# Weight casts on ScalarE: one by one in the norms, four in the cross attention, token-major copies ahead of squares

## The chip, the cores and the metric

The kernel runs on one core of a Trainium2 chip. The metric is the device time of one execution in microseconds (us); smaller is better. Three runs of the kernel before took 1008.64, 1008.8 and 1011.63 us, so the median is 1008.8 us.

The engines are TensorE (PE in the profile, with PEld for its weight loads), VectorE (DVE), ScalarE (ACT), GpSimd (POOL) and SyncE (SP), which only issues transfers here. Each works through its own instructions in order, and waits on semaphores for the others.

## The reference

Two transformer blocks run one after the other on 256 tokens of width 1024, in fp32:

```
first block:   u = rms_norm(h); proj = u @ w_in
               y_a = softmax attention of 8 heads (RoPE)          [moba, att]
               y_b = gated delta rule of 8 heads, in chunks       [conv, tok, feat, inv, scan]
               h += rms_norm((sig(ga)*(y_a@w_proj_a) + sig(gb)*(y_b@w_proj_b)) @ w_out)     norm "mix"
               h += rms_norm((silu(f@w_gate) * (f@w_up)) @ w_down)                          norm "ffn1"
               h += sigmoid(h @ w_ple_gate) * e                                             norm "ple"
second block:  x += rms_norm(concat(diff attention, pooling) @ w_out_2)                     norm "mix2"
               x += rms_norm(cross_attention(rms_norm(x)@w_xq, mem) @ w_xo)                 norm "x"
               x += rms_norm((silu(f@w_gate_2) * (f@w_up_2)) @ w_down_2)                    norm "ffn2"
```

The names at the right are the kernel's for the places where a product's rows are normed, added to the residual and made ready for the next product. The gated delta rule needs its q and k normed over the 128 dimensions of a head, so their squares are summed; `tok` is the step that does it.

## The kernel before, in words

Each fp32 product is computed in three passes: weights and activations are split into a high and a low half (`w_hi`, `w_lo`, `uH`, `uL`), and PE computes high x high (L505), high x low weight (L506) and low x high weight (L507). The 2 x 128 tokens (t = 0, 1) are the stationary side, 512 columns of weights the moving side; the results lie in eight PSUM banks, L0 to L3 for the large products and Q0 to Q3 for turned (transposed) tiles.

The weights come as 294 units of 128 x 1024 numbers (512 KB). Every unit takes four stations:

- SP loads it into one of four `raw` places. Unit n waits until the low half of unit n - 4 is made, since that frees its place.
- ACT casts it to `w_hi` (L1257). This cast waits for the load, and for PE to be done with the unit that held the `w_hi` place before.
- POOL subtracts, two instructions a unit, to `w_lo` (L495).
- PE uses it.

The order of all this is written out by hand. `schedule()` lists the steps, and each engine's function goes through them. ACT does the casts between its other work, at the points where the code says `split_past`, `split_up_to` or `split_freed`. `split_freed(step, j)` makes all casts that need no more of PE than that unit j of that step is used up; for what was already made it does nothing. What the code puts behind such a call waits, on ACT, until those casts are done, and so for their loads.

A norm between two products is spread over three engines. The names below are those of the code, each for token tile t and column half c:

- ACT `row_sum` squares a PSUM bank and sums it (L1348, tile `hg`; in norm "ple" it is a sigmoid on L1346). It waits for the bank.
- DVE `gained` (L1885), `root` (L1818, seven small instructions), `added` (L1903) and `scaled` (L1914, writes `hg`).
- PE `turn_half` turns that half (L722, four instructions).
- ACT `kept` copies the residual out of PSUM (L1332), and `hi_half` casts the turned half to `uH` (L1269). DVE `lo_half` subtracts to `uL` (L1851). The next product's matmuls on this half (L505) wait for it, in `wait_low`; `bank_free` makes them wait for `kept` too.

PE calls the first `turn_half` of a norm just ahead of the last nine matmuls of the product before it (`row_tail`, TAIL = 5 units for t = 1). These nine are the only work that PE has while ACT and DVE do the high and the low half.

In the cross attention (`cross`), ACT copies turned probabilities (`cross_probs`, L1320) and casts the attention's output to `uH` (`cross_hi`, L1326), while PE computes values and already a part of `xo`, the product behind it. In `tok`, PE turns 3 parts (q, k, v) x 2 token tiles through banks Q0 to Q2 (L920), ACT copies each out (L1450) and squares q and k (L1459), and DVE sums the squares (L2010). A bank is turned into again when its copy is out.

Of the kernel before, what the change touches and what calls it, by code (L numbers as in the profile page):

```python
# [26 lines left out]
ACT = mybir.ActivationFunctionType  # L27
# [4 lines left out]
NT = SEQ // P  # L32
# [3 lines left out]
GH = 4  # L36
# [125 lines left out]
TAIL = 5  # L162
# [57 lines left out]
def build(nc, a, out, known):  # L220
# [30 lines left out]
    with ctx:  # L251
# [986 lines left out]
        def _(act):  # L1238
# [146 lines left out]
            def fill(step, i):  # L1385

                split_up_to(FIRST[FILLING[step][0]] + i + SPLIT)
# [5 lines left out]
            for step in SCHEDULE:  # L1393
# [50 lines left out]
                elif kind == "tok":  # L1444
                    for part in range(3):
                        for t in range(NT):
                            act.wait_ge(*PE(step, "turned", part, t))
                            if part == 0 and t == 0 and step[1] == 1:
                                act.wait_ge(*PE(("scan", 0), "o", 1))
                            copy(tok[:, t, part, :, :], Q[(part * NT + t) % 3][:].rearrange("p (h d) -> p h d", h=GH)).then_inc(*AC.mark(step, "out", part, t))  # L1450
                            if t == 0:
                                fill(*((step, part - 1) if part else (("decay", step[1]), 3)))
                            if part < 2:
                                act.wait_ge(*AC(step, "out", part, t))
                                if part > 0:
                                    act.wait_ge(*VE(step, "sum", part - 1, t))
                                elif step[1] == 1:
                                    act.wait_ge(*VE(("scan", 0), "sum", t))
                                actf(sq[t][:], tok[:, t, part, :, :], ACT.Square).then_inc(*AC.mark(step, "sq", part, t))  # L1459
                    fill(step, 2)  # L1460
# [141 lines left out]
                elif kind == "norm":  # L1602
# [6 lines left out]
                    if what == "ffn2":  # L1609
                        row_sum(what, 2)  # L1610
                        row_sum(what, 3)
                        continue
                    split_freed(src_step, last - 3)
                    if pre:
                        kept(what, 0, 0)
                elif kind == "next":
# [3 lines left out]
                    pre = RES[what][1]  # L1620
                    hi_half(step, 0, 0)
                    row_sum(what, 2)
                    row_sum(what, 3)
                    if pre:
                        kept(what, 0, 1)
# [150 lines left out]
                elif kind == "cross":  # L1776
# [9 lines left out]
                    cross_hi(0)  # L1786
                    cross_probs(1)
                    cross_hi(1)
                elif kind == "xo":
# [610 lines left out]
```

## Time and profile before

| | |
|---|---|
| median of three runs | 1008.8 us |
| the profiled execution | 1008.19 us |
| its span, first to last instruction | 1006.4 us |
| PE busy | 974.2 us, 97% |
| POOL busy | 741.9 us, 74% |
| ACT busy | 512.1 us, 51% |
| DVE busy | 366.0 us, 36% |
| mean granted clock of PE | 0.994 of full speed |

The span covers the program's instructions; some 1.8 us lie around it. "Busy" is time in which an engine executes something; a matmul's end is modelled, so that rows of consecutive matmuls overlap. In a timeline row the figure in brackets is how long the engine sat idle before the row, with what ended that.

### The profile page before, as it was taken

How to read it: one execution, taken by the hardware profiler on the slowest of the kernel's cores; microseconds unless marked ns; L12 is line 12 of the kernel's file. 1: busy time of each engine (PE TensorE's matmuls, PEld its weight loads, DVE VectorE, ACT ScalarE, POOL GpSimd, SP SyncE). 2: the span in 40 equal slices, each digit the busy share in tenths (PEclk: the TensorE clock that was granted, in tenths of full speed). 3: DMA queues.
4: the chain of work that ended last, by engine and by line, in shares of the span. 5: the costliest groups of instructions: out<-in, count | busy, mean ns of one | idle time of the engine just before them, and what ended most of it. 6: DMA issues, size and time to landing. Idle time of an engine off the chain costs nothing.

```text
span 1006.4 us, 15320 instructions
## 1 busy us (share of the span) xinstructions
PE 974.2 (97%) x6004; PEld 830.0 (82%) x6004; DVE 366.0 (36%) x840; ACT 512.1 (51%) x759; POOL 741.9 (74%) x592
## 2 busy tenths in 40 slices
PE   5999999999999999999999998999999899999997
PEld 5988889988888887888898876899888778888885
DVE  4677434776524235112122244143253161111103
ACT  5376624465524446465444554575556465444431
POOL 6868543876632987999976976868976579888890
PEclk9999999999999999999999999999999999999999
DMA  8546231555332775667654665645655357666541
GB/s 262 177 129 206 85 112 61 179 154 167 106 107 84 235 246 167 212 201 210 189 167 148 195 205 166 220 149 170 190 189 164 95 159 227 188 189 187 180 136 42
DMA packets 76752, 167.37 MB, mean 166 GB/s; under 512 B 8348, under 2 KB 13704, under 8 KB 76552
## 3 DMA queue, kind: packets, MB, share of 16 engines
q1 hardware_dynamic: 71296, 156.40, 50.6%
q10 hardware_dynamic: 5384, 9.99, 3.0%
q8 instruction: 47, 0.77, 0.3%
q14 instruction: 25, 0.20, 0.1%
HBM read 165.32 MB, written 1.05 MB: 165 GB/s over the span
## 4 chain that ended last, share of the span: by engine, by line
PE 84%; POOL 5%; ACT 3%; DVE 3%; DMA 2%; issue 1%; DVEq 0%; ACTq 0%
PE L L505 19%; PE L L507 19%; PE L L506 18%; POOL w_lo L495 5%; PE L L865 2%; PE Q L507 2%; PE Q L505 2%; PE Q L506 2%; PE L L867 2%; PE L L866 2%; ACT w_hi L1257 1%; PE Q L1034 1%; PE Q L1016 1%; PE Q L722 1%; DMA raw<-in_w_in 1%
## 5 line engine op out<-in xcount | busy, mean ns | idle before, releaser
L495 POOL TENSOR_TENSOR w_lo<-raw,w_hi 128x512 fp32r<-128x512 f32 x588 | 741.7, 1299 | 238.9 <-ACT w_hi L1257 238.3
L1257 ACT CAST w_hi<-raw 128x1024 fp32r<-128x1024 f32 x294 | 304.9, 1053 | 259.6 <-PE L L507 103.9
L505 PE MATMUL L<-w_hi,uH 128*128 128x512 f32 (+1 forms) x768 | 306.0, 398 | 6.3 <-DVE uL L1851 6.0
L507 PE MATMUL L<-w_hi,uL 128*128 128x512 f32 (+1 forms) x768 | 297.3, 387 | 0.0
L506 PE MATMUL L<-w_lo,uH 128*128 128x512 f32 (+1 forms) x768 | 296.8, 386 | 0.0
L505 PEld LDWEIGHTS L<-w_hi,uH 128*128 128x128 f32 x768 | 145.1, 189 | 37.8 <-DVE uL L1851 9.5
L507 PEld LDWEIGHTS L<-w_hi,uL 128*128 128x128 f32 x768 | 144.8, 189 | 30.0
L506 PEld LDWEIGHTS L<-w_lo,uH 128*128 128x128 f32 x768 | 145.2, 189 | 27.0 <-issue 0.5
L505 PE MATMUL L<-w_hi,hH 128*128 128x512 f32 x176 | 69.0, 392 | 0.0
L507 PE MATMUL L<-w_hi,hL 128*128 128x512 f32 x176 | 68.6, 390 | 0.0
L506 PE MATMUL L<-w_lo,hH 128*128 128x512 f32 x176 | 68.5, 389 | 0.0
L1812 DVE TENSOR_TENSOR hL<-Q,hH 128x512 fp32r<-128x512 f32 x22 | 15.2, 692 | 121.3 <-ACT hH L1669 120.9
L865 PE MATMUL L<-uH,w_hi 128*128 128x256 f32 x192 | 55.0, 287 | 0.9 <-DVE baH L1969 0.8
L866 PE MATMUL L<-uL,w_hi 128*128 128x256 f32 x192 | 54.4, 284 | 0.0
L867 PE MATMUL L<-uH,w_lo 128*128 128x256 f32 x192 | 54.4, 283 | 0.0
L1885 DVE TENSOR_TENSOR L<-L,gA 128x512 f32<-128x512 f32 x20 | 14.0, 699 | 97.3 <-ACT hg L1348 96.8
L1818 DVE TENSOR_SCALAR small<-small 128x1 f32<-128x1 f32 (+1 forms) x177 | 39.0, 220 | 24.1 <-ACT xv L1593 13.1
L1851 DVE TENSOR_TENSOR uL<-Q,uH 128x512 fp32r<-128x512 f32 x28 | 19.3, 691 | 64.3 <-ACT uH L1269 64.3
L1821 DVE SCALAR_TENSOR_TENSOR hm<-L,small,sil 128x512 f32<-128x512 f32 x20 | 15.0, 751 | 65.7 <-PE L L507 65.3
L507 PEld LDWEIGHTS L<-w_hi,hL 128*128 128x128 f32 x176 | 33.0, 188 | 7.0
L506 PEld LDWEIGHTS L<-w_lo,hH 128*128 128x128 f32 x176 | 33.1, 188 | 6.7
L505 PEld LDWEIGHTS L<-w_hi,hH 128*128 128x128 f32 x176 | 33.1, 188 | 6.6
(335 smaller groups left out, 1281.8 us busy)
## 6 DMA issues: line engine op xcount, KB each, us to landing
raw<-in_w_in SPq DMA_DIRECT2D x88, 512.0 KB, 3.6
raw<-in_w_ffn_gate SPq DMA_DIRECT2D x22, 512.0 KB, 3.7
raw<-in_w_ffn_up SPq DMA_DIRECT2D x22, 512.0 KB, 3.7
raw<-in_w_ffn_down SPq DMA_DIRECT2D x22, 512.0 KB, 3.5
raw<-in_w_gate SPq DMA_DIRECT2D x22, 512.0 KB, 3.6
raw<-in_w_up SPq DMA_DIRECT2D x22, 512.0 KB, 3.6
raw<-in_w_down SPq DMA_DIRECT2D x22, 512.0 KB, 3.5
raw<-in_w_out SPq DMA_DIRECT2D x16, 512.0 KB, 3.5
```

The costliest lines, as they stand in the source:

```text
L495: last = nc.gpsimd.tensor_tensor(lo[:, cc], raw[:, n % RAW, cc], hi[:, cc].bitcast(F32), ALU.subtract)
L505: mm(dst, sH, wH, start=start, stop=False)
L506: mm(dst, sH, wL, start=False, stop=False)
L507: return mm(dst, sL, wH, start=False, stop=stop)
L865: mm(bank, sH, uH[:, k, :], start=k == 0, stop=False)
L866: mm(bank, sH, uL[:, k, :], start=False, stop=False)
L867: last = mm(bank, sL, uH[:, k, :], start=False, stop=k == KD - 1)
L1257: copy(halves[SLOT[u]][0], raw[:, u % RAW, :]).then_inc(w_hi_there, 1)
L1812: v(V.tensor_tensor(out_, x_, y_, op), *name)
L1818: v(V.tensor_scalar(out_, x_, s1, s2_, op0, op1), *name)
L1821: v(V.scalar_tensor_tensor(out=out_, in0=x_, scalar=s_, in1=y_, op0=op0, op1=op1), *name)
L1851: vector_next(V.tensor_tensor(uL[:, 4 * half:4 * half + 4, t * P:(t + 1) * P], heads(Q[2 * t + half]), uH[:, 4 * half:4 * half + 4, t * P: ...
```

## The change

Three edits, all in the ACT function. PE, DVE, POOL and SP keep their instructions and their order.

1. `tok`: the copies and squares, written as a loop before, are written out. The copy of (part 1, t 0) now stands ahead of the squares of (part 0, t 1), where it stood behind.
2. The norms: `split_freed(src_step, last - 3)` ahead of the first `kept` made three casts in a row. Now `last - TAIL` makes one there; the second stands behind the first `hi_half`, and the third behind the row sums of t = 1. This holds for the norms "mix", "ffn1", "ple", "mix2" and "x"; "ffn2", the last, has no casts.
3. `cross`: `split_freed(values, 3)` is added between the second `cross_probs` and the second `cross_hi`. It makes four casts, which the step `xo` made before.

```diff
--- before.py
+++ after.py
@@ -1442,21 +1442,33 @@
                         if t == 0:
                             fill(step, 2)
                 elif kind == "tok":
-                    for part in range(3):
-                        for t in range(NT):
-                            act.wait_ge(*PE(step, "turned", part, t))
-                            if part == 0 and t == 0 and step[1] == 1:
-                                act.wait_ge(*PE(("scan", 0), "o", 1))
-                            copy(tok[:, t, part, :, :], Q[(part * NT + t) % 3][:].rearrange("p (h d) -> p h d", h=GH)).then_inc(*AC.mark(step, "out", part, t))
-                            if t == 0:
-                                fill(*((step, part - 1) if part else (("decay", step[1]), 3)))
-                            if part < 2:
-                                act.wait_ge(*AC(step, "out", part, t))
-                                if part > 0:
-                                    act.wait_ge(*VE(step, "sum", part - 1, t))
-                                elif step[1] == 1:
-                                    act.wait_ge(*VE(("scan", 0), "sum", t))
-                                actf(sq[t][:], tok[:, t, part, :, :], ACT.Square).then_inc(*AC.mark(step, "sq", part, t))
+                    def token_major(part, t):
+                        act.wait_ge(*PE(step, "turned", part, t))
+                        if part == 0 and t == 0 and step[1] == 1:
+                            act.wait_ge(*PE(("scan", 0), "o", 1))
+                        copy(tok[:, t, part, :, :], Q[(part * NT + t) % 3][:].rearrange("p (h d) -> p h d", h=GH)).then_inc(*AC.mark(step, "out", part, t))
+
+                    def squares(part, t):
+                        act.wait_ge(*AC(step, "out", part, t))
+                        if part > 0:
+                            act.wait_ge(*VE(step, "sum", part - 1, t))
+                        elif step[1] == 1:
+                            act.wait_ge(*VE(("scan", 0), "sum", t))
+                        actf(sq[t][:], tok[:, t, part, :, :], ACT.Square).then_inc(*AC.mark(step, "sq", part, t))
+
+                    token_major(0, 0)
+                    fill(("decay", step[1]), 3)
+                    squares(0, 0)
+                    token_major(0, 1)
+                    token_major(1, 0)
+                    squares(0, 1)
+                    fill(step, 0)
+                    squares(1, 0)
+                    token_major(1, 1)
+                    squares(1, 1)
+                    token_major(2, 0)
+                    fill(step, 1)
+                    token_major(2, 1)
                     fill(step, 2)
                     fill(step, 3)
                 elif kind == "moba":
@@ -1610,7 +1622,7 @@
                         row_sum(what, 2)
                         row_sum(what, 3)
                         continue
-                    split_freed(src_step, last - 3)
+                    split_freed(src_step, last - TAIL)
                     if pre:
                         kept(what, 0, 0)
                 elif kind == "next":
@@ -1619,8 +1631,10 @@
                     last = KF if src_step[0] == "down" else KD
                     pre = RES[what][1]
                     hi_half(step, 0, 0)
+                    split_freed(src_step, last - TAIL + 1)
                     row_sum(what, 2)
                     row_sum(what, 3)
+                    split_freed(src_step, last - TAIL + 2)
                     if pre:
                         kept(what, 0, 1)
                     hi_half(step, 0, 1)
@@ -1785,6 +1799,7 @@
                     values_out(3, [Q[2], Q[3]])
                     cross_hi(0)
                     cross_probs(1)
+                    split_freed(values, 3)
                     cross_hi(1)
                 elif kind == "xo":
                     split_freed(step, KD - TAIL - 1)
```

How the change moves instructions, as the two programs' ACT orders show it (a number behind an x is how often the row repeats; numbers behind `w_hi` name a tile outside the first six places).

First the norm "mix". `hg,small<-L` are the row sums, `h<-L` is `kept`, `uH<-Q` is `hi_half`. Before:

```order
L1348 ACTIVATE hg,small<-L 128x512 x2
L1257 CAST w_hi<-raw 128x1024 x3
L1332 COPY h<-L 128x512
L1269 CAST uH<-Q 128x4x128
L1348 ACTIVATE hg,small<-L 128x512 x2
L1332 COPY h<-L 128x512
L1269 CAST uH<-Q 128x4x128
```

After:

```order
L1348 ACTIVATE hg,small<-L 128x512 x2
L1257 CAST w_hi<-raw 128x1024
L1332 COPY h<-L 128x512
L1269 CAST uH<-Q 128x4x128
L1257 CAST w_hi<-raw 128x1024
L1348 ACTIVATE hg,small<-L 128x512 x2
L1257 CAST w_hi<-raw 128x1024
L1332 COPY h<-L 128x512
L1269 CAST uH<-Q 128x4x128
```

Two of three casts have moved behind the first high half, one of them on behind the second pair of row sums. "ffn1" (which has no `kept`), "ple" and "mix2" move alike.

Second the end of the cross attention, `xo` and the norm "x". The first row is `cross_hi` of t = 1 before, the first cast after; the tiles 130 and 132 are places lent from the memory's buffers. Before:

```order
L1326 CAST uH<-Q 128x4x128 x2
L1257 CAST w_hi<-raw 128x1024 x2
L1257 CAST w_hi_130<-raw 128x1024
L1257 CAST w_hi_132<-raw 128x1024
L1257 CAST w_hi<-raw 128x1024 x2
L1257 CAST w_hi_138<-raw 128x1024
L1348 ACTIVATE hg,small<-L 128x512 x2
L1257 CAST w_hi_140<-raw 128x1024
L1257 CAST w_hi<-raw 128x1024 x2
L1332 COPY h<-L 128x512
L1269 CAST uH<-Q 128x4x128
```

After:

```order
L1257 CAST w_hi<-raw 128x1024 x2
L1257 CAST w_hi_130<-raw 128x1024
L1257 CAST w_hi_132<-raw 128x1024
L1326 CAST uH<-Q 128x4x128 x2
L1257 CAST w_hi<-raw 128x1024 x2
L1257 CAST w_hi_138<-raw 128x1024
L1348 ACTIVATE hg,small<-L 128x512 x2
L1257 CAST w_hi_140<-raw 128x1024
L1332 COPY h<-L 128x512
L1269 CAST uH<-Q 128x4x128
L1257 CAST w_hi<-raw 128x1024
L1348 ACTIVATE hg,small<-L 128x512 x2
```

Seven casts stood between `cross_hi` and the norm's row sums; now three do, and four stand ahead of `cross_hi`.

Third the start of `tok`, group 0. `tok<-Q` is a copy, `sq<-tok` a square. Before:

```order
L1450 COPY tok<-Q 128x512
L1459 ACTIVATE sq_90<-tok 128x512
L1450 COPY tok<-Q 128x512
L1459 ACTIVATE sq_91<-tok 128x512
L1450 COPY tok<-Q 128x512
L1257 CAST w_hi<-raw 128x1024
```

After:

```order
L1449 COPY tok<-Q 128x512
L1457 ACTIVATE sq_90<-tok 128x512
L1449 COPY tok<-Q 128x512 x2
L1457 ACTIVATE sq_91<-tok 128x512
L1257 CAST w_hi<-raw 128x1024
```

The third copy has moved ahead of the second square.

## Rows read from the trace of the kernel before

**Rows 1.** The page: span, and the busy time of PE

```profile
span 1006.4 us, 15320 instructions
PE 974.2 (97%) x6004; PEld 830.0 (82%) x6004; DVE 366.0 (36%) x840; ACT 512.1 (51%) x759; POOL 741.9 (74%) x592
```

**Rows 2.** Waits of PE, whole span: line, waited for, us in total, times, longest

```profile
PE L L505 <- DVE uL L1851: 6.0, 4, 2.8
PE Q L722 <- DVE hg L1914: 5.4, 2, 5.0
```

**Rows 3.** Timeline of PE, idle rows: start, us, what, [idle <-releaser]

```profile
75.48 0.63 PE L920 MATMUL Q<-table,C 128*128 128x128 f32 x4 [0.51 <-ACT tok L1450]
...
388.57 0.50 PE L505 MATMUL L<-w_hi,uH 128*128 128x512 f32 x1 [1.85 <-DVE uL L1851]
...
585.10 0.50 PE L505 MATMUL L<-w_hi,uH 128*128 128x512 f32 x1 [1.10 <-DVE uL L1851]
...
611.90 0.50 PE L505 MATMUL L<-w_hi,uH 128*128 128x512 f32 x1 [2.78 <-DVE uL L1851]
...
807.21 1.11 PE L722 MATMUL Q<-table,hg 128*128 128x128 f32 x4 [5.03 <-DVE hg L1914]
...
811.70 0.50 PE L505 MATMUL L<-w_hi,uH 128*128 128x512 f32 x1 [0.30 <-DVE uL L1851]
```

**Rows 4.** Timeline of PE, norm "mix": the turned half

```profile
384.02 0.60 PE L722 MATMUL Q<-table,hg 128*128 128x128 f32 x4
```

**Rows 5.** Timeline of ACT, norm "mix": third cast, high half

```profile
385.70 1.05 ACT L1257 CAST w_hi<-raw 128x1024 fp32r<-128x1024 f32 x1 [1.01 <-DMA raw<-in_w_ffn_up]
...
387.13 0.59 ACT L1269 CAST uH<-Q 128x512 fp32r<-128x512 f32 x1
```

**Rows 6.** Timeline of POOL, norms "mix", "ple", "mix2"; two instructions are a unit

```profile
376.95 15.01 POOL L495 TENSOR_TENSOR w_lo<-raw,w_hi 128x512 fp32r<-128x512 f32 x12 [3.81 <-ACT w_hi L1257]
...
599.36 14.97 POOL L495 TENSOR_TENSOR w_lo<-raw,w_hi 128x512 fp32r<-128x512 f32 x12 [4.75 <-ACT w_hi L1257]
...
734.52 1.30 POOL L495 TENSOR_TENSOR w_lo<-raw,w_hi 128x512 fp32r<-128x512 f32 x1 [1.34 <-ACT w_hi L1257]
```

**Rows 7.** Windows: length, busy of PE, PEld, DVE, ACT, POOL, granted clock, DMA share, GB/s

```profile
612.00:615.00 3.00, 3.00 (x11) 2.35 (x11) 1.84 (x3) 0.61 (x2) 2.33 (x2) 0.57 0.60 219
615.00:618.00 3.00, 3.00 (x14) 2.44 (x13) 1.98 (x3) 2.71 (x4) 1.09 (x1) 0.86 0.60 186
...
807.20:811.70 4.50, 4.20 (x13) 3.20 (x13) 1.44 (x3) 3.04 (x7) 4.50 (x5) 0.65 0.74 217
```

**Rows 8.** Timeline of ACT, cross attention to norm "x"

```profile
778.51 1.08 ACT L1320 COPY cpT<-Q 128x512 f32<-128x512 f32 x2
786.82 0.59 ACT L1326 CAST uH<-Q 128x512 fp32r<-128x512 f32 x1 [7.23 <-PE Q L840]
...
789.09 3.89 ACT L1257 CAST w_hi<-raw 128x1024 fp32r<-128x1024 f32 x4
796.36 1.05 ACT L1257 CAST w_hi<-raw 128x1024 fp32r<-128x1024 f32 x1 [3.38 <-DMA raw<-in_w_gate]
...
802.33 0.58 ACT L1348 ACTIVATE hg<-L 128x512 f32<-128x512 f32 x1
```

**Rows 9.** Timeline of POOL, cross attention to the next product

```profile
768.22 7.52 POOL L495 TENSOR_TENSOR w_lo<-raw,w_hi 128x512 fp32r<-128x512 f32 x6 [3.12 <-ACT w_hi L1257]
790.22 24.86 POOL L495 TENSOR_TENSOR w_lo<-raw,w_hi 128x512 fp32r<-128x512 f32 x20 [14.49 <-ACT w_hi L1257]
```

**Rows 10.** Timeline of ACT, norm "mix2": first row sum

```profile
722.40 0.60 ACT L1348 ACTIVATE hg<-L 128x512 f32<-128x512 f32 x1 [4.00 <-PE L L507]
```

**Rows 11.** Timeline of PE, norm "mix2": its first turned half

```profile
727.65 0.60 PE L722 MATMUL Q<-table,hg 128*128 128x128 f32 x4
```

**Rows 12.** Timeline of ACT, `tok` of group 0: second square, third copy

```profile
74.23 0.63 ACT L1459 ACTIVATE sq<-tok 128x512 f32<-128x512 f32 x1
74.77 0.57 ACT L1450 COPY tok<-Q 128x512 f32<-128x512 f32 x1
```

## The prediction, on record before the kernel after was run

> **What bounds the kernel now.** I read four views. The page comes first: PE is busy 974.2 of 1006.4 us [rows 1], so only its 32 idle us can be won by a change that leaves PE's instructions as they are. Second the waits of PE: apart from the start and the end of the kernel, it waits 6.0 us for low halves `uL` and 5.4 us for normed rows `hg` [rows 2]; low weight halves from POOL are not among PE's waits. Third the timeline of PE, which places them: 0.51 us in `tok`, then 1.85, 1.10 and 2.78 us in the norms "mix", "ffn1" and "ple", each just before the next product's first matmul, and in the norm "x" 5.03 us before its first turned half and 0.30 us behind it [rows 3]. These six are 11.6 us. Fourth the timelines of ACT and POOL around them, for what ACT did meanwhile.
>
> **The high half behind three casts.** In "mix" PE turned the first half from 384.02 to 384.62 [rows 4]. ACT could have cast it then, but its third weight cast stood ahead: it waited for a load until 385.70, and the high half began at 387.13 [rows 5]. `uL` came 1.4 us later, and PE, out of work at 388.57 - 1.85 = 386.72, went on at 388.57 [rows 3]. In the changed order one cast stands ahead, and it is made while DVE still works on the rows. The high half starts at about 384.65, 2.5 us earlier, and `uL` is there at 387.13 - 2.5 + 1.4 = 386.05, 0.7 us before PE needs it. So the 1.85 us go. "ffn1" and "ple" have the same pattern, with waits of 1.10 and 2.78 us. In "ple" the third cast waited for its load longest, so the most goes there; PE starts its turn, as in "mix" (386.72 - 384.02), 2.7 us before it runs dry, and the turn, the hand-over, the high and the low half need 0.6 + 0.05 + 1.4 = 2.05 us of that. In "mix2" PE shows no such wait, and I put 0 there. Sum of the norms' low-half waits: 1.85 + 1.10 + 2.78 = 5.73 us.
>
> **The four casts.** ACT is idle for 7.23 us ahead of the first `cross_hi` of t = 1 at 786.82, and behind the second one it makes four casts in 3.89 us from 789.09 [rows 8]. POOL, with nothing to subtract, has been idle for 14.49 us by 790.22 [rows 9], and as only its subtraction frees a `raw` place, the loads stand still too: the fifth cast waits 3.38 us for its load [rows 8]. With two more such waits behind it, ACT comes to the row sums at 802.33 [rows 8]. How late is that? In "mix2", where no cast stands in the way, row sum and turned half begin at 722.40 and 727.65, 5.25 us apart [rows 10, 11]. In "x" PE was ready to turn at 807.21 - 5.03 = 802.18, so its row sum could have begun at 802.18 - 5.25 = 796.9; it began 5.4 us late, which is the wait of 5.03 us [rows 3]. In the new order the four casts start when `cross_probs` ends, at 779.6, and end at 783.5, 3.3 us ahead of `cross_hi` at 786.82 [rows 8]. All four loads are there: POOL made three units from 768.22 to 775.74 [rows 9], and the last load was free to start when it ended, 6.7 us before the fourth cast begins at 782.5. POOL goes from 780.7, at 2.49 us a unit (24.86 us for 10 [rows 9]), and has made four units by 790.7. The three casts that still stand ahead of the row sums need loads that start at 783.2, 785.7 and 788.2 and the first three `xo` units used up by PE, the last of them at about 794.5 (eleven pieces of three matmuls follow it before 802.18; nine matmuls took 386.72 - 384.62 = 2.1 us in "mix", so these take 7.7). They end by 796, the row sum begins near 796.9, and the 5.03 us go. The 0.30 us behind are again a high half behind two casts, and go as in "mix".
>
> **The clock.** After the two longest waits PE's granted clock is down: 0.57 of full speed in 612 to 615, 0.86 in 615 to 618, 0.65 in 807.2 to 811.7 [rows 7], that is, 1.2 GHz for part of each window and 2.4 for the rest. That cost 3.0 x 0.43 + 3.0 x 0.14 = 1.7 us in "ple" and 4.5 x 0.35 = 1.6 us in "x". Where the wait is gone the fall should be gone: 3.3 us. After 1.85 and 1.10 us the windows show nothing to win.
>
> The Trainium skill ("TensorE: Matmul & The Clock Gate", section "What's actually happening") speaks against counting on this: the activity window runs free of the kernel, so when the clock changes differs from run to run. By that rule a fall can come at another wait of the changed kernel, or have been missing in some runs of the kernel before. The trace has one execution and can't show which.
>
> **`tok`.** PE's turn at 75.48 waited 0.51 us for the copy at 74.77, which stood behind the square of 74.23 [rows 3, 12]. The copy moves up by the square's 0.54 us and the wait goes. The square and its sum on DVE come 0.5 us later; the next square waits for its own copy behind a cast anyway, so this costs nothing. If DVE's sums were on the path it would be 0.5 us a group, and the edit worth 0. Group 1 shows no wait: 0.
>
> **What the moved casts may cost.** Each cast that moves back is hidden only while POOL still has units in hand. In "mix" POOL runs six units without a pause from 376.95 in 15.01 us [rows 6], 2.50 us each, so it takes the fifth (the cast that moves behind the high half) at 386.95; the cast will end at about 386.2. The margin is 0.75 us. In "ple" it takes its fifth at 599.36 + 10.0 = 609.3 [rows 6], and the cast ends near 608.6: 0.7 us. PE needs that unit's low half about 0.5 us after it is made, in "mix" and in "ple". In "mix2" the cast comes some 3 us later than now, after POOL has run out, so POOL falls back 1.8 us; but it idles 1.34 us before 734.52 [rows 6], and PE uses that unit some 3 us after it is made. Cost 0 at the forecast. The other new thing is that the second residual copy and high half now stand behind a cast of 1.05 us [rows 5]. PE and the next DVE steps had 0.4 to 0.7 us to spare there by my count. I take 0.1 us for each of four norms, 0.4 in all; the bounds are 0 and 1.05 x 4 = 4.2 us. Below nothing it can hardly go, except that the first matmul after a wait takes 0.50 us [rows 3], longer than those behind it: I allow 0.1 us at five places.
>
> **Sum.** 0.51 + 5.73 + 5.03 + 0.30 + 3.3 - 0.4 = 14.5 us, all on PE's own path. The profiled execution took 1008.19 us, 0.6 under the median of 1008.8, so 993.7 in its terms and 994.3 us for the median.
>
> **The rivals.**
> - *The waits move one place on.* The second high half, now behind a cast, or the residual copy that frees its bank, makes PE wait instead. For it: the margins of half a microsecond. Against it: the cast is short and its load is already there. Price up to 4.2 us: 998.5.
> - *The four casts don't help "x".* Their loads or places come late, or the three casts left still reach the row sums. For it: the loads there have been the slowest of all, 3.38 us [rows 8]. Against: that wait followed from POOL's pause, which goes. Then 5.03 + 0.30 + 1.6 = 6.9 us are missing: 1001.2.
> - *The clock falls somewhere all the same.* The time is 3.3 us longer: 997.6.
> - *The change doesn't do what it says.* The one cast left ahead of the copies waits as long as the three did. That cast needs only the unit that PE uses up first behind the row sums, well before the turn, so this is unlikely. Only the 0.51 us and "x" remain: 1001.
> - *Slower: POOL runs dry.* Two casts are moved back in each norm. If each reached POOL too late for PE, PE would wait at most for one cast and two subtractions, 1.05 + 2.50 = 3.55 us [rows 5, 6]; twice in four norms that is 28.4 us, so 994.3 + 28.4 = 1022.7. It decides from 14.5 / 8 = 1.8 us per moved cast. The margins of 0.7 us ahead of POOL and 0.5 behind it would have to be wrong by 3 us.
>
> **How the numbers follow.** The forecast has 0.76, moved waits 0.10, no help in "x" 0.05, the clock 0.04, change without effect in the norms 0.02, slower 0.03. A measurement of this kernel tells no change from one of 0.3% (3 us) at best. All cases but the last are faster by more; I leave 0.03 to no difference, for errors of my reading that cancel the gain, and take them from the forecast: faster 0.94, same 0.03, slower 0.03. The forecast's own range is 992.8 (no new waits, and the slow first matmuls won) to 996. The range for 8 in 10 reaches to the first and third rival: 992 to 999.
>
> **What the new profile would show.** No idle row of PE over 0.2 us at `tok`'s turns and before the first L505 of the products after "mix", "ffn1" and "ple"; in each norm the high half within 0.1 us of the end of the four L722. ACT's four casts start about 1 us after the second `cross_probs` begins and end before `cross_hi`; POOL's pause of 14.49 us shrinks to about 5; the first row sum of "x" begins about 5.3 us before PE's first L722 there, with no idle time before that. The clock stays at 1.00 through "ple" and "x".  I am wrong if PE shows a new wait over 1 us for `w_lo`, for `h` or for a low half of the second column half, or if the row sums of "x" still come after casts that wait for loads.

## The result, and the profile after

The changed kernel takes 992.12 us (median of four runs, 992.07 to 992.29). The kernel before, run beside it, took 1009.45 us (four runs, 1008.64 to 1011.63, the three of above among them). The ratio is 0.9825, with a 95% interval of 0.9808 to 0.9842. The forecast was 994.3 us; the ratio times 1008.8 us is 991.1 us, 0.9 below the low end of the range. So the kernel became faster, as forecast, and by more than the range allowed. The margin hangs on the kernel before: the 992.12 us themselves are 2.2 under the forecast, and the rest comes in because its median was 1009.45 us beside this run. The same kernel measured again (e4 below) has the ratio 0.984, which makes 992.7 us, just inside the range.

The page of the kernel after, its span and its busy times, beside [rows 1]:

```profile
span 990.3 us, 15320 instructions
PE 970.0 (98%) x6004; PEld 828.4 (84%) x6004; DVE 366.4 (37%) x840; ACT 511.5 (52%) x759; POOL 742.4 (75%) x592
```

The span is 16.1 us shorter. PE's busy time fell by 4.2 us as well, with the same 6004 matmuls, so not all of the gain is waiting that went: some matmuls took less time. Its mean granted clock rose from 0.994 to 0.997 of full speed.

All waits of PE in the kernel after (line, waited for, us in total, times, longest), beside [rows 2]:

```profile
PE L L887 <- DMA small<-in_ln_pre_mix: 6.5, 1, 6.5
PE Q L705 <- DVE xn L1972: 3.7, 2, 2.6
PE L L865 <- DVE baH L1984: 0.6, 1, 0.6
PE Q L722 <- DVE hg L1929: 0.4, 1, 0.4
```

The first three lie in the first 20 us of the kernel, which the change doesn't touch. The line for `uL` is gone, and of the two waits for `hg` [rows 2] the one of 5.0 us; the other, 0.4 us in "ple", is left. The timelines show how. First the norm "mix": ACT, DVE and PE in the kernel after, beside [rows 3 to 5]:

```profile
382.80 0.59 ACT L1332 COPY h<-L 128x512 f32<-128x512 f32 x1 [1.73 <-DVE hg L1929]
383.80 0.59 ACT L1269 CAST uH<-Q 128x512 fp32r<-128x512 f32 x1 [0.41 <-PE Q L722]
384.28 1.05 ACT L1257 CAST w_hi<-raw 128x1024 fp32r<-128x1024 f32 x1
385.24 0.60 ACT L1348 ACTIVATE hg<-L 128x512 f32<-128x512 f32 x1
...
386.48 1.04 ACT L1257 CAST w_hi<-raw 128x1024 fp32r<-128x1024 f32 x1
```

```profile
383.17 0.60 PE L722 MATMUL Q<-table,hg 128*128 128x128 f32 x4
383.52 0.48 PE L505 MATMUL L<-w_hi,uH 128*128 128x512 f32 x1
...
385.46 0.40 PE L507 MATMUL L<-w_hi,uL 128*128 128x512 f32 x1
385.69 0.39 PE L505 MATMUL L<-w_hi,uH 128*128 128x512 f32 x1
```

The high half at 383.80 starts 0.03 us behind the turn, which ends at 383.77. The last nine matmuls of the product start between 383.52 and 385.46, and the first matmul of the next product (385.69) follows with no idle time. The casts at 384.28 and 386.48 find their loads there, so they hold up nobody. And POOL doesn't run out of work although they have moved. Its timeline through "mix" in the kernel after, and through the cross attention, beside [rows 6, 9]:

```profile
376.10 20.08 POOL L495 TENSOR_TENSOR w_lo<-raw,w_hi 128x512 fp32r<-128x512 f32 x16 [3.70 <-ACT w_hi L1257]
...
759.45 7.51 POOL L495 TENSOR_TENSOR w_lo<-raw,w_hi 128x512 fp32r<-128x512 f32 x6 [3.12 <-ACT w_hi L1257]
771.84 9.98 POOL L495 TENSOR_TENSOR w_lo<-raw,w_hi 128x512 fp32r<-128x512 f32 x8 [4.88 <-ACT w_hi L1257]
785.11 10.05 POOL L495 TENSOR_TENSOR w_lo<-raw,w_hi 128x512 fp32r<-128x512 f32 x8 [3.29 <-ACT w_hi L1257]
```

In "mix" it makes eight units without a pause. In the cross attention the pause of 14.49 us has become two, of 4.88 and 3.29 us, with four units made between them. ACT there, beside [rows 8]:

```profile
770.70 3.91 ACT L1257 CAST w_hi<-raw 128x1024 fp32r<-128x1024 f32 x4
778.05 0.59 ACT L1326 CAST uH<-Q 128x512 fp32r<-128x512 f32 x1 [3.44 <-PE Q L840]
...
783.99 3.10 ACT L1257 CAST w_hi<-raw 128x1024 fp32r<-128x1024 f32 x3 [3.56 <-PE L L507]
788.01 0.60 ACT L1348 ACTIVATE hg<-L 128x512 f32<-128x512 f32 x1 [0.93 <-PE L L507]
```

PE's first turned half in "x":

```profile
793.26 0.60 PE L722 MATMUL Q<-table,hg 128*128 128x128 f32 x4
```

The four casts end 3.4 us ahead of `cross_hi`. The next three wait for a place that PE uses up (3.56 us), and no longer for a load, and the row sum at 788.01 waits for PE's own bank. PE turns the half at 793.26, 5.25 us later, with no idle time before it.

Last the clock. Windows of the kernel after (length, busy of PE, PEld, DVE, ACT, POOL, granted clock, DMA share, GB/s), through "ple" and "x", beside [rows 7]:

```profile
604.00:607.00 3.00, 2.90 (x16) 2.16 (x15) 2.09 (x4) 2.86 (x6) 3.00 (x3) 1.00 0.66 208
607.00:610.00 3.00, 3.00 (x15) 2.46 (x14) 2.34 (x4) 1.76 (x3) 3.00 (x3) 1.00 0.73 227
...
792.00:796.00 4.00, 4.00 (x21) 3.29 (x20) 2.90 (x6) 2.69 (x6) 3.65 (x4) 1.00 0.76 240
```

**Where the 16.1 us came from.** PE's instructions are the same and stand in the same order in both kernels, so instruction k of the one can be laid beside instruction k of the other, and the difference of their start times, followed through the program, shows each place where the kernel after gains:

| place | gain, us | forecast: wait, clock | what was not in the forecast |
|---|---|---|---|
| start of the kernel | 0.2 | | 0.2 |
| `tok` | 0.66 | 0.51 | 0.15 |
| "mix" | 2.16 | 1.85 | 0.31 |
| "ffn1" | 1.34 | 1.10 | 0.24 |
| "ple" | 4.37 | 2.78 + 1.7 | -0.11 |
| "x" | 7.35 | 5.03 + 0.30 + 1.6 | 0.42 |
| new waits | 0 | -0.4 | 0.4 |
| sum | 16.1 | 14.5 | 1.6 |

The 0.2 us at the start aren't the change's: in the other traces of these experiments, PE at `tok` lies between 0.0 and 0.3 us from the kernel before, whatever was edited. The row of "ffn1" also holds 0.06 us that were lost between "mix" and "ffn1".

Where the last column comes from can be seen at "mix". In the kernel before PE's last matmul ahead of the wait is this:

```profile
386.32 0.40 PE L507 MATMUL L<-w_hi,uL 128*128 128x512 f32 x1
```

The next one started at 388.57 [rows 3], 2.25 us later; in the kernel after the same two start at 385.46 and 385.69, 0.23 us apart. So the wait delayed PE by 2.02 us, where its row says 1.85: the idle time is counted from the modelled end of a matmul, 0.40 us behind its start, while without a wait the next would have started after 0.23. That is 0.17 us that the idle row leaves out. The first matmul behind the wait then took 0.50 us instead of 0.39, another 0.11. The rest of the 0.31, some 0.03 us, lies in the matmuls behind. In `tok` the wait's 0.15 us are the first part alone.

In "ple" the same parts are there, but one thing goes the other way. PE in the kernel after, ahead of its second turned half:

```profile
605.72 0.39 PE L507 MATMUL L<-w_hi,uL 128*128 128x512 f32 x1
606.21 0.66 PE L722 MATMUL Q<-table,hg 128*128 128x128 f32 x4
```

The two start 0.49 us apart, 0.26 more than the usual 0.23: at its full clock PE comes to this turn before DVE has written the rows (its row ends at 606.15). In the kernel before, PE was slowed there by its clock and came later. This small new wait is too short to stand in the list of waits, and is inside the row of "ple" in the table.

### The profile page after: what moved, and what is told of

It reads as the page before. It is cut to its first block, busy times and chain, and to the rows that moved or that the text cites. A ratio compares the mean times of both kernels' runs of the same rounds, so it can differ in the third digit from the quotient of the medians.

```text
span 990.3 us, 15320 instructions
## 1 busy us (share of the span) xinstructions
PE 970.0 (98%) x6004; PEld 828.4 (84%) x6004; DVE 366.4 (37%) x840; ACT 511.5 (52%) x759; POOL 742.4 (75%) x592
## 4 chain that ended last, share of the span: by engine, by line
PE 96%; DVE 2%; DMA 1%; ACT 1%; issue 0%; POOL 0%; DVEq 0%
PE L L505 22%; PE L L507 22%; PE L L506 22%; PE L L865 2%; PE L L866 2%; PE L L867 2%; PE Q L507 2%; PE Q L505 2%; PE Q L506 2%; PE Q L1034 1%; PE Q L722 1%; PE Q L1016 1%; PE Q L1114 1%; PE L L776 1%; PE L L778 1%; PE L L777 1%
```

## The experiments

Each run was timed beside the kernel before on its own chip; the medians of before were 1008.41 us (first four experiments), 1008.83 (e5 to e8) and 1009.2 (e9, e10).

**Each edit alone.** The first four experiments take the change apart.

```diff
 e1: before +
-                    split_freed(src_step, last - 3)
+                    split_freed(src_step, last - TAIL)
...
+                    split_freed(src_step, last - TAIL + 1)
...
+                    split_freed(src_step, last - TAIL + 2)
```

> The kernel before with edit 2 alone (casts one by one in the five norms). Theory (each PE wait is won by the edit that stands at its place, and the clock comes back with it): gone are 1.85 us in mix, 1.10 in ffn1, 2.78 plus 1.7 of clock in ple, and the slow first matmuls, together 2.16 + 1.34 + 4.4 = 7.9 us by the trace of after; the 5 us wait in x and the 0.51 in tok stay. Span 1006.4 - 7.9 = 998.5. Rival (the gain hangs together: what is won in a norm is only kept because POOL and the loads are also ahead from the cross attention): span above 1000. In both the clock falls once, behind the wait in x.

```diff
 e2: before +
                     cross_probs(1)
+                    split_freed(values, 3)
                     cross_hi(1)
```

> The kernel before with edit 3 alone (four casts between the second probabilities' copies and the second high halves of the cross attention). Theory: the 5.03 us wait in x and its clock fall go, 6.6 us; the 0.30 us behind it may stay, since the first high half there still stands behind casts, and with it up to 0.7. Span 999.1 to 999.8. Rival (in x the casts inside the norm would hold up the high half now that it is on time): a new wait of 1 to 3 us for the low half in x, span 1001 to 1003.

```diff
 e3: before +
-                    for part in range(3):
...
+                    token_major(0, 1)
+                    token_major(1, 0)
+                    squares(0, 1)
...
```

> The kernel before with edit 1 alone (token-major copies ahead of squares). Theory: the wait of 0.51 us goes, span 1005.7 to 1005.9. Rival: the wait moves to DVE's later sums, span 1006.4.

e4 is the changed kernel once more, on the chip of e1 to e3; its diff is empty.

> The kernel after once more, on the same chip as the three parts. Theory (the parts add up, as they lie at different places of PE's path): its saving in span is the sum of the three parts' within 0.5 us. Rival: the whole saves at least 1 us more than the sum, as in x edit 2 and edit 3 work on the same wait. Second question, the spread: the runs of before lie 3 us apart and those of after 0.2. If the spread comes from how the clock falls at long PE waits, each kernel that keeps such a wait has a spread of 1 us or more, and this one none.

| | median (lowest to highest), us | to before | ratio |
|---|---|---|---|
| e1, the norms | 1000.35 (1000.08 to 1000.8) | -8.06 | 0.9922 [0.9907, 0.9937] |
| e2, the cross attention | 1002.85 (1000.37 to 1004.03) | -5.56 | 0.9938 [0.9921, 0.9955] |
| e3, `tok` (ten runs) | 1007.87 (1006.61 to 1010.21) | -0.54 | 0.9995 [0.9986, 1.0005] |
| e4, all three | 992.13 (991.99 to 992.35) | -16.28 | 0.984 [0.9825, 0.9855] |

e4 repeats the result. The norms and the cross attention each carry their share, the norms as expected (spans of 998.3 to 999.0 us in four runs, 998.5 expected); `tok` alone can't be told from no change by its time. In its trace, whose span is 1.6 us shorter than that of before with 0.66 of them in `tok` (the rest lies at the start and at waits that differ from execution to execution), all twelve turning matmuls stand in one row, with no idle time; in the kernel before four came behind 0.51 us [rows 3]. PE in `tok` of e3:

```profile
73.37 1.79 PE L920 MATMUL Q<-table,C 128*128 128x128 f32 x12
```

The parts make 14.2 us, the whole 16.3. So the second of e4's two cases came (the whole saves over 1 us more than the sum), and two of the traces show where 2.1 us can come from. With the norms changed alone, the long wait in "x" stays, and the clock is at its lower level behind it. PE in e1, and the windows behind:

```profile
799.34 1.11 PE L722 MATMUL Q<-table,hg 128*128 128x128 f32 x4 [5.01 <-DVE hg L1916]
```

```profile
801.00:804.00 3.00, 3.00 (x8) 2.32 (x8) 2.21 (x4) 1.71 (x4) 3.00 (x3) 0.50 0.72 191
804.00:807.00 3.00, 3.00 (x15) 2.40 (x14) 0.54 (x1) 2.64 (x6) 1.69 (x2) 0.86 0.74 228
```

The low stretch is longer here than in the kernel before: a whole window at 0.50 where that had 4.5 us at 0.65 [rows 7]. Followed instruction by instruction, e1 loses 0.45 us in "x" against the kernel before, although the second wait there, of 0.30 us, is gone.

With the cross attention changed alone, PE's start in "x" is on time, but the high half there still stands behind casts: waits for `uL` are 7.1 us in all, 1.1 more than in [rows 2], of which 0.77 us are in "x". e2 gains 6.25 us in "x". With the 0.45 that e1 loses, the two edits alone make 5.8 us there; together they make 7.3. So they need each other in "x" for 1.5 us.

The rest has nothing to do with "x". The wait in "ffn1", of 1.10 us in [rows 3], was 1.80 us in this execution of e2, with the clock down behind it; that lost 2.25 us against the kernel before. Its span of 1002.2 us lies in the rival's range of 1001 to 1003, but not for the rival's reason (a wait of 1 to 3 us in "x"). It is the slowest of e2's four executions; the fastest had a span of 998.6, 0.5 below the theory's 999.1. PE and windows in e2:

```profile
585.63 0.50 PE L505 MATMUL L<-w_hi,uH 128*128 128x512 f32 x1 [1.80 <-DVE uL L1852]
```

```profile
584.00:587.00 3.00, 1.37 (x6) 1.12 (x7) 2.05 (x3) 1.95 (x6) 3.00 (x4) 0.97 0.69 220
587.00:590.00 3.00, 3.00 (x11) 2.41 (x10) 1.56 (x7) 0.28 (x1) 2.00 (x2) 0.50 0.51 177
```

That is the 1.2 GHz level over a whole window, behind a wait as long as that of "mix" in the kernel before, behind which I had seen nothing. In 587 to 590 PE ran at half its speed, which costs 3.0 x 0.50 = 1.5 us. The forecast had put this cost at nothing for waits of this length; e6 and e9 return to it.

**What makes "x" faster.** The theory was that the row sums are late because casts that wait for loads stand ahead of them. The rival: what counts is that POOL and the loads start early. e5 takes the four early casts back, and puts the first two row sums of "x" ahead of the casts in another way.

```diff
-                    split_freed(src_step, last - TAIL)
+                    split_freed(src_step, last - TAIL - (what == "x"))
...
-                    split_freed(values, 3)
...
-                    split_freed(step, KD - TAIL - 1)
+                    split_freed(("xkv", 3), 3)
```

> The kernel after, with the four casts back behind the second high halves of the cross attention, but the norm x's first two row sums ahead of the three casts that wait for loads (units 230 to 232), and the fourth behind the first high half. Theory (x lost its 5 us only because row sums stood behind casts that waited for loads): POOL still pauses 14 us, but PE's turn comes on time; span within 0.5 us of after's 990.3. Rival (POOL and the loads had to start earlier): PE waits 1 us or more in x, for a low half behind the casts or for w_lo, and the span is 991.5 to 994.

It took 996.55 us (995.99 to 996.66), ratio 0.9877 [0.986, 0.9895], 4.4 us more than the changed kernel; its span of 994.8 us is even above the rival's 991.5 to 994. The 5 us ahead of PE's turn are gone and the first low half is in time, so the order on ACT alone does that. But POOL's pause is back, and PE now waits six matmuls behind its second turned half. PE, with a window behind the wait, then ACT and POOL in e5 (POOL's row goes on past the stretch that was asked for, here and in e7):

```profile
801.71 0.50 PE L505 MATMUL L<-w_hi,uH 128*128 128x512 f32 x1 [2.53 <-ACT h L1332]
```

```profile
804.00:807.00 3.00, 3.00 (x10) 2.37 (x10) 2.70 (x6) 1.85 (x2) 3.00 (x3) 0.66 0.73 236
```

```profile
797.57 1.05 ACT L1257 CAST w_hi<-raw 128x1024 fp32r<-128x1024 f32 x1 [1.34 <-DMA raw<-in_w_up]
...
800.13 1.04 ACT L1257 CAST w_hi<-raw 128x1024 fp32r<-128x1024 f32 x1 [0.34 <-DMA raw<-in_w_up]
801.08 0.58 ACT L1332 COPY h<-L 128x512 f32<-128x512 f32 x1
```

```profile
781.50 18.79 POOL L495 TENSOR_TENSOR w_lo<-raw,w_hi 128x512 fp32r<-128x512 f32 x15 [14.49 <-ACT w_hi L1257]
```

The residual copy that frees PE's bank stands behind a cast whose load is late, and the load is late since POOL is. Of the 4.4 us, 2.8 are this wait and PE's start behind it, and 1.6 are the clock, which fell behind it (0.66 of full speed in 804 to 807). So both theories hold, each for a part: the order on ACT decides whether the first half comes in time, the early casts decide whether the loads do. Of the first rival of the forecast ("the residual copy that frees its bank makes PE wait") this is the picture; it comes about when the loads are late, not by the order itself.

e10 asks how many early casts are needed: two of the four.

```diff
-                    split_freed(values, 3)
+                    split_up_to(NUMBER[("xo",), KD - 1] + 1)
```

> The kernel after, with two of the four casts ahead of the second high halves of the cross attention and the other two behind them in xo. Theory (what counts is that the loads of the three casts ahead of the row sums have started): the loads of units 230 and 231 start early, that of 232 starts when POOL has done unit 228, late, so that its cast ends about when the row sum could begin; PE waits 0 to 0.6 us at its turn in x; span 990.3 to 991.2. Rival (all four are needed): the row sums come 2.5 us late or more; span 993 or above.

992.49 us (992.38 to 992.64), ratio 0.9833 [0.9817, 0.985]: 0.4 us more than the changed kernel. One cast still waits for its load ahead of the row sums. ACT in e10:

```profile
787.89 1.05 ACT L1257 CAST w_hi<-raw 128x1024 fp32r<-128x1024 f32 x1 [1.67 <-DMA raw<-in_w_up]
788.84 0.59 ACT L1348 ACTIVATE hg<-L 128x512 f32<-128x512 f32 x1
```

That makes the row sum 0.8 us later than in the kernel after (788.01), of which 0.2 us were there before the cross attention, and PE's turn in "x" 0.3 us later on its own account. The other 0.2 us of the profiled execution were lost in the first 75 us, which this edit doesn't touch. So two early casts bring nearly all, and the other two 0.3 us.

**How much room the moved casts have.** e7 puts the second cast behind the row sums of t = 1 and the third to the next place after.

```diff
                     hi_half(step, 0, 0)
-                    split_freed(src_step, last - TAIL + 1)
                     row_sum(what, 2)
                     row_sum(what, 3)
-                    split_freed(src_step, last - TAIL + 2)
+                    split_freed(src_step, last - TAIL + 1)
```

> The kernel after, with the second cast of each norm behind the row sums of t = 1, and the third with it. This puts it later by two row sums, 1.2 us, or more where the last sum waits for PE; POOL takes that unit 1.2 to 1.7 us after the one before is finished. Theory of the margins (0.7 us ahead of POOL, 0.5 us behind it): PE now waits for w_lo in mix and in ple, 0.5 to 1.3 us each, and not in ffn1, mix2 and x; span 991.3 to 992.9. Rival (the order behind the first high half is free, all that matters is that it is not behind three casts): 990.3.

995.59 us (995.05 to 996.02), ratio 0.9869 [0.9854, 0.9884]: 3.5 us more than the changed kernel. In PE's waits of e7, norms now wait for the low weight halves of POOL, which the kernel after never does; POOL's timeline in "mix" is in the second fence:

```profile
PE L L505 <- POOL w_lo L495: 2.0, 2, 1.2
PE Q L722 <- DVE hg L1928: 1.1, 2, 0.7
...
PE L L505 <- ACT h L1332: 0.3, 1, 0.3
```

```profile
387.73 6.29 POOL L495 TENSOR_TENSOR w_lo<-raw,w_hi 128x512 fp32r<-128x512 f32 x5 [1.44 <-ACT w_hi L1257]
```

POOL runs dry for 1.44 us there, and PE waits 1.2 us for `w_lo`. So the slower rival's mechanism is real, and the margin of under 1 us per cast, worked out in the forecast from POOL's rows, was about right: one place later costs. It costs more than was expected before the run (a span of 991.3 to 992.9; it was 994.2), since in "ple" PE also waits 0.71 us for `hg` and in "mix2" 0.30 us for `h`. The profiled execution, at 996.02 us the slowest of the four, took 3.9 us more than that of the kernel after. The waits of `w_lo`, `hg` and `h` make 3.0 of them beyond the 0.4 there; followed instruction by instruction, another 0.2 to 0.3 us lie at each of the three longer waits, as in the table of gains, and 0.1 at the start.

**The clock, and the spread of the runs.** e6 gives "ple" its old order back, e9 "mix".

```diff
 e6 (e9: "mix" for "ple")
-                    split_freed(src_step, last - TAIL)
+                    split_freed(src_step, last - (3 if what == "ple" else TAIL))
```

> The kernel after, with the three casts in a row put back in the norm ple alone. Theory: PE waits 2.5 to 2.8 us there again, and its clock falls behind it: span 990.3 + 4.4 = 994.7 in an execution like that of before. Spread theory (where the clock falls after such a wait differs from run to run): its runs lie 0.5 us or more apart, while after's lie 0.4 apart. Rival to the clock part: the slow matmuls of before came with something else there, and only the wait of 2.8 comes back: 993.1, without spread.

> The kernel after, with the three casts in a row put back in the norm mix alone. Theory: PE waits 1.7 to 1.9 us there again, and with its restart the span is 990.3 + 2.1 = 992.4 where the clock holds. Spread theory (the clock falls behind a wait of this size in some executions and not in others): the runs lie 0.5 us or more apart, the highest up to 2 us above the lowest. Rival (only waits over 2.5 us bring a fall): runs as close as after's, 0.4 us.

e6: 995.55 us (995.36, 995.39, 995.72, 996.84), ratio 0.9872 [0.9856, 0.9888], 3.4 us more than the changed kernel, of which the trace has 2.57 us for `uL` and a second wait of 0.41 us for `hg`. e9: 995.39 us (994.38, 994.90, 995.87, 996.27), ratio 0.9862 [0.9847, 0.9877], 3.3 us more. Each has its old wait back, and in both profiled executions the clock stays up behind it. So e6's span is 993.6 us, nearer to the 993.1 of the rival without a fall than to 994.7, while its runs lie 1.5 us apart, as the spread theory says. PE and one window in e6, then in e9:

```profile
607.44 0.50 PE L505 MATMUL L<-w_hi,uH 128*128 128x512 f32 x1 [2.57 <-DVE uL L1866]
...
609.51 0.66 PE L722 MATMUL Q<-table,hg 128*128 128x128 f32 x4 [0.41 <-DVE hg L1929]
```

```profile
607.40:611.00 3.60, 3.14 (x15) 2.37 (x16) 2.10 (x4) 1.55 (x4) 2.71 (x3) 1.00 0.54 201
```

```profile
387.82 0.50 PE L505 MATMUL L<-w_hi,uH 128*128 128x512 f32 x1 [1.78 <-DVE uL L1866]
```

```profile
388.00:391.00 3.00, 3.00 (x16) 2.44 (x17) 2.17 (x4) 1.77 (x5) 3.00 (x3) 1.00 0.73 212
```

The profiled execution of e9 took 994.38 us. Against the changed kernel's 992.14 that is 2.24 us, of which 2.1 lie at the wait of 1.78: the wait and 0.3 us for starting again, as the table of gains has it (1.85 + 0.31). But it was the fastest of the four. The others took up to 1.9 us more, while the kernel after, which has no wait left in the norms but one of 0.4 us and the short one of 0.26, lies within 0.2 us over four runs, and within 0.4 us in e4.

What the spread consists of is not seen in e9's one trace. Other runs tell more. Each execution has a mean granted clock beside its time. A thousandth or two of it mean nothing by themselves: the kernel after has 0.997 to 0.999 in four runs 0.2 us apart, because the clock also falls behind PE's last matmul. Larger differences go with the time. e2's four executions took 1000.37, 1002.31, 1003.39 and 1004.03 us, at 0.999, 0.997, 0.994 and 0.995. Of the thirteen of the kernel before, the eight at 0.994 or 0.995 took 1007.23 to 1008.63 us, the five at 0.991 or 0.993 took 1008.67 to 1010.07. So in these two kernels most of the spread goes with the clock. For e9 the same (0.997 for its two faster executions, 0.996 for the slower two) is too coarse to show it: there it is argued.

The twelve traces also show behind which waits of PE the clock fell, those of the kernels' first 21 us left out:

| idle time of PE, us | in | the clock fell |
|---|---|---|
| 4.95 to 5.03 | before, e1, e3 | 3 of 3 times |
| 2.53 to 2.80 | before, e2, e3, e5, e6 | 4 of 5 times (not in e6) |
| 1.68 to 1.85 | before, e2 (twice), e3, e9 | once of 5 (the 1.80 us of e2) |
| 1.21 and less | all | never |

So a wait of 5 us has cost its stretch of low clock each time, one of 2.5 to 2.8 us mostly, and one of under 2 us once. e1 fits this: it keeps one wait of 5 us, and its four runs lie only 0.7 us apart, all at 0.995.

**The wait that is left.** e8 keeps the change and reorders DVE in "ple": `added` and `scaled` of the last half stand ahead of the low half of the half before.

```diff
+                    if what == "ple":
+                        added(what, 1, 1)
+                        scaled(what, 1, 1)
+                        lo_half(step, 1, 0)
+                    else:
                         lo_half(step, 1, 0)
                         added(what, 1, 1)
                         scaled(what, 1, 1)
```

> The kernel after, with DVE in the norm ple doing the last quarter's sum and scaling ahead of the low half of t = 1, where it idles 1.4 us or more. Theory: PE's wait of 0.41 us for hg there goes, and nothing comes for it: span 989.9, median 991.7. Rival: the low half comes later and PE waits for that: 990.3 or more.

991.55 us (991.51 to 991.64), ratio 0.9829 [0.9815, 0.9844]. It is 0.57 us less than the changed kernel took, and the ranges of their four runs don't overlap; in the traces 0.63 us lie at this place. DVE sat idle for 3.16 us there in the kernel after, and the three steps for the last half came behind it; in e8 they fill that time. DVE in "ple", first the kernel after, then e8:

```profile
613.51 0.69 DVE L1866 TENSOR_TENSOR uL<-Q,uH 128x512 fp32r<-128x512 f32 x1 [3.16 <-ACT uH L1269]
...
615.58 0.69 DVE L1929 TENSOR_TENSOR hg<-L,gB 128x512 f32<-128x512 f32 x1
```

```profile
611.95 0.69 DVE L1929 TENSOR_TENSOR hg<-L,gB 128x512 f32<-128x512 f32 x1
613.60 0.69 DVE L1866 TENSOR_TENSOR uL<-Q,uH 128x512 fp32r<-128x512 f32 x1 [0.96 <-ACT uH L1269]
```

## Why the prediction was right in its mechanisms and short in its sum

- *The high half behind three casts.* Right, 5.73 us of waits went in "mix", "ffn1" and "ple"; e1 has them gone with the norms' edit alone, and e6 and e9 bring two of them back one by one. The high half came 0.03 us behind the turn, where "within 0.1 us" stood.
- *The four casts.* Right, with its working: row sum to turn 5.25 us, and no idle time. (In the kernel before the same stretch took only 4.88 us, from 802.33 to 807.21, which is why a row sum 5.4 us late made a wait of 5.03.) That the four would start at 779.6 of the old time was right as well (770.70, in a kernel that is 8.7 us ahead by then). POOL's pause became 4.88 and 3.29 us, where one of about 5 was told. e5 shows that the order was not enough, and that the step through POOL and the loads was needed.
- *The margins.* Right: no wait for `w_lo` in the kernel after, and one as soon as the casts move a place on (e7). So the slower case didn't come, though its mechanism exists.
- *`tok`.* Right: 0.66 us in the trace; in the timed runs (e3) it can't be told from nothing.
- *Starting again.* The failed step, first part, and the largest: the sum priced each wait at its idle row alone. Matched instruction by instruction, the waits that went were worth 1.0 us more than their idle rows and the clock term: 0.15 in `tok`, 0.31 in "mix", 0.24 in "ffn1", 0.42 for the two in "x", and -0.11 in "ple". Some 0.14 to 0.17 us of each is the overlap of matmuls that an idle row leaves out; 0.11 more is the slow first matmul, where it has 512 columns. The rows of the kernel before had both. I had allowed 0.1 us at five places, and only in the range.
- *New waits.* The failed step, second part: I took 0.4 us for the casts that now stand ahead of the second high halves, and these cost nothing. The one new wait is the 0.26 us in "ple", which comes of PE's full clock; in e6, which has the old order of casts in "ple", it is there as well, with 0.41 us of idle time (609.51). The other 0.41 us for `hg` in "ple" are no new wait: they are the second of the two in [rows 2], stay in every other kernel here but e8, and e8 shows that DVE's order makes them.
- *The clock, and the step from the profiled execution to the median.* The failed step, third part, 0.6 us. The clock term itself (3.3 us for "ple" and "x") was right in its mechanism and about in its size: the clock stays at 1.00 there, and in "x" that was worth 1.5 us of the 1.6. But the forecast took the 0.6 us between the profiled execution and the median of before for something around every kernel, and added it to the time after. For the kernel after that difference is 0.02 us (992.14 to 992.12). And "After 1.85 and 1.10 us the windows show nothing to win" read one execution as if it were all: in the profiled ones there was nothing to win, but e2 has the lower level behind 1.80 us. The slower executions of before are those with the lower clock, so they were part of what the change removes.
- *The range.* Its own low end was given as 992.8, for no new waits and the slow first matmuls won; 994.3 - 0.4 - 0.5 makes 993.4.

The sums then close. In the profiled executions 14.5 + 1.0 + 0.4 + 0.2 = 16.1 us; the last 0.2, at the start of the kernel, are chance. With the 0.6 us of the last step that makes the 2.2 us from 994.3 to 992.12. The medians beside the result differ by 1009.45 - 992.12 = 17.3 us, and the 1.2 us more are the distance of before's median from its profiled execution of 1008.19 us. With the other medians of before (1008.41 to 1009.2) it is 16.3 to 17.1 us. So it is luck on which side of 992 us the ratio puts the result; that the sum was 1.6 us short is not.

The prediction cited the Trainium skill ("TensorE: Matmul & The Clock Gate", section "What's actually happening") for an activity window that runs free of the kernel, so that the moment of a clock change differs from run to run. The runs agree that it differs: waits of 2.78 us (before) and 2.57 us (e6) in the same place had the clock at 0.57 and at 1.00 behind them. The forecast used that rule only against the gain (a fall at some other wait). It speaks for it as well: a kernel with waits pays for them in some of its executions, and a change that takes the waits away earns this.

What stays open: how often the clock falls behind a wait of 1 to 2 us (once in five here is too few to say), and so how the 1.2 us divide between the waits. That would take many traces of one kernel.

## What to carry to other kernels

An engine that works in order should do what another engine waits for as soon as its input is there, and put work that may itself wait for a load behind it, as long as the consumer of that work (here POOL) still has more in hand than the delay; e7 shows that this stock was worth under one place. A pause of the engine that frees the load buffers is paid for later, at the first instruction that stands behind a cast whose load is late, so look for idle time upstream to put such work in (e5, e10). When the engine that bounds the kernel loses a wait, count more than its idle time. Take the distance between the starts of the two instructions, less the usual distance, instead of the idle row; add the slow first matmul, and the clock in those executions where it falls. A spread of 2 us between runs of this kernel was itself a sign that there was something to win; the reverse doesn't hold, since e1 has a wait of 5 us and a spread of 0.7.

## What the runs showed of the hardware

- Behind a wait PE's first matmul of 512 columns took 0.50 us, and 0.39 us in a row of its like; right behind a turn, with no wait, it took 0.48 (383.52). Matmuls of 512 columns start 0.23 us apart at full clock while each one's row lasts 0.39 to 0.40, so that an idle row is some 0.17 us shorter than the delay.
- The granted clock fell to 0.50, the 1.2 GHz level, behind a wait of 1.80 us (e2), and stayed at 1.00 behind waits of 1.78 (e9) and 2.57 us (e6). It fell at all three waits of about 5 us, at four of five from 2.5 to 2.8, at one of five from 1.7 to 1.85, and at none of 1.21 us or less.
- In those kernels whose waits in the norms are gone (the changed one, e8, e10) four runs lie within 0.1 to 0.4 us; with one such wait back within 1.5 (e6) and 1.9 us (e9), and with several, in the kernel before, within 2.8 us (thirteen runs, 1007.23 to 1010.07).
